# A two-layer hybrid trunk: block attention in pairs of heads with the values stationary, the r and k products first, the memory's keys of layer 0 projected inside the group norm

## What is computed

```python
# layer 0: RWKV-7 time mixing
dx = shift(h) - h
xr, xw, xk, xv, xa, xg = [h + dx * mu[s] for s in range(6)]
r = xr @ w_rkv[0]; k = xk @ w_rkv[1]; v = xv @ w_rkv[2]
w = -softplus(-(w0 + tanh(xw @ w1) @ w2)) - 0.5      # decay, low rank 64
a = sigmoid(a0 + (xa @ a1) @ a2)                      # rate, low rank 64
g = sigmoid(xg @ g1) @ g2                             # gate, low rank 128
o = scan over the tokens(r, decay, k, v, kk, a)       # 16 heads of 64
o = group_norm(o) * lnx_g + lnx_b                     # per head
x = x + ((o + bonus) * g) @ w_o
# both layers: cross-attention into 256 memory tokens, 4 heads of 256
kv = rms_norm(mem, ln_memkv[i]) @ w_kv                # keys and values
x = x + softmax(q k^T / 16) v @ w_o,  q = rms_norm(x, ln_mem[i]) @ w_q
# layer 1: block attention, 16 heads of 64, blocks of 256 tokens, rotary q and k
p = softmax(q k^T / 8, causal);  o = p v;  x = x + o @ w_o
```

## Time and profile before

| | us |
|---|---|
| median of 3 runs | 2491.16 (2490.17 to 2491.65) |
| the profiled execution's own time | 2486.15 |
| its span | 2484.3 |
| TensorE busy | 2130.0 (86%), mean granted clock 0.943 |
| VectorE busy | 621.0 (25%) |
| ScalarE busy | 413.8 (17%) |
| chain that ended last | PE 67%, DMA 21% (expert weights 19%), DVE 5%, issue of transfers 4%, ACT 1% |

### The profile page before, as it was taken

The page is one execution under the profiler, slowest core; times in us unless marked ns, Lnnn a source line. Parts: engine busy times, 40 slices in busy tenths (PEclk is TensorE's granted clock), DMA queues, the critical chain, the costliest instruction groups (busy, mean ns, idle before and its releaser), DMA issues.

```text
span 2484.3 us, 33316 instructions
## 1 busy us (share of the span) xinstructions
PE 2130.0 (86%) x14314; PEld 1120.0 (45%) x14314; DVE 621.0 (25%) x1388; ACT 413.8 (17%) x1003; POOL 198.4 (8%) x237
## 2 busy tenths in 40 slices
PE   6899999959999688778775999999999788877773
PEld 2345799935554422222222445766455322222221
DVE  5301655561022311000012420631022311000003
ACT  3202233320021011000001102621021010000001
POOL 1000121010000111111010000000000111111110
PEclk9999899979999799998898999999999899999997
DMA  4010000022324699999998122003324799999995
GB/s 137 34 68 34 11 4 4 4 85 71 132 71 169 240 401 404 406 402 409 409 403 341 35 97 73 1 26 110 119 71 167 310 402 405 408 406 408 396 410 212
DMA packets 113071, 515.08 MB, mean 207 GB/s; under 512 B 20736, under 2 KB 21896, under 8 KB 95536
## 3 DMA queue, kind: packets, MB, share of 16 engines
q1 hardware_dynamic: 101824, 496.34, 51.1%
q0 software_dynamic: 10880, 16.81, 2.1%
q10 hardware_dynamic: 240, 0.07, 0.0%
HBM read 503.73 MB, written 28.31 MB: 214 GB/s over the span
## 4 chain that ended last, share of the span: by engine, by line
PE 67%; DMA 21%; DVE 5%; SPq 4%; ACT 1%; issue 1%; POOLq 0%; DVEq 0%; POOL 0%; ACTq 0%
DMA big<-in_moe_w 19%; PE ps L1632 11%; PE ps L1645 11%; PE ps L2049 11%; PE ps L1740 9%; PE ps L1977 4%; SPq L471 4%; PE ps L2070 3%; PE ps L1691 2%; PE ps L1889 1%; PE ps L1881 1%; PE ps L1942 1%; PE ps L1854 1%; PE ps L1954 1%; PE ps L1860 1%
## 5 line engine op out<-in xcount | busy, mean ns | idle before, releaser
L2049 PE MATMUL ps<-big 128*64 128x512 f32 x2048 | 475.7, 618 | 73.7 <-DMA big<-in_moe_w 72.0
L2049 PEld LDWEIGHTS ps<-big 128*64 128x64 f32 x2048 | 163.0, 142 | 337.2 <-issue 326.2
L1632 PE MATMUL ps<-big 128*128 128x512 f32 (+1 forms) x768 | 279.4, 526 | 6.6 <-issue 6.6
L2070 PE MATMUL ps<-big 128*64 128x512 f32 x1024 | 255.9, 646 | 31.1 <-ACT big L1002 31.1
L1645 PE MATMUL ps<-big 128*128 128x512 f32 x640 | 275.5, 592 | 0.0
L1632 PEld LDWEIGHTS ps<-big 128*128 128x128 f32 x768 | 147.4, 193 | 136.8 <-issue 128.6
L1740 PE MATMUL ps<-big 64*64 64x64 f32 (+1 forms) x6144 | 203.1, 223 | 6.2 <-DVE big L1166 3.6
L1740 PEld LDWEIGHTS ps<-big 64*64 64x64 f32 x6144 | 198.1, 135 | 8.6 <-DVE big L1166 3.7
L1645 PEld LDWEIGHTS ps<-big 128*128 128x128 f32 x640 | 121.6, 190 | 151.3 <-issue 151.1
L1524 DVE SCALAR_TENSOR_TENSOR big<-big,ps 128x256 f32<-128x256 f32 x64 | 27.0, 422 | 530.2 <-ACT big L995 530.2
L2070 PEld LDWEIGHTS ps<-big 128*64 128x64 f32 x1024 | 73.4, 146 | 172.4 <-issue 134.1
(11 more groups left out here) (316 smaller groups left out, 1943.6 us busy)
## 6 DMA issues: line engine op xcount, KB each, us to landing
big<-in_moe_w SPq DMA_DIRECT2D x192, 2048.0 KB, 33.8
big<-in_mx_wkv SPq DMA_DIRECT2D x8, 2048.0 KB, 7.9
big<-in_rw_wrkv SPq DMA_DIRECT2D x6, 2048.0 KB, 8.0
big<-in_mb_wqkv SPq DMA_DIRECT2D x6, 2048.0 KB, 8.0
big<-in_mx_wq SPq DMA_DIRECT2D x4, 2048.0 KB, 7.9
big<-in_mx_wo SPq DMA_DIRECT2D x4, 2048.0 KB, 8.1
h_rows<-big SPq DMA_DIRECT2D x16, 512.0 KB, 12.5
big<-y_rows SPq DMA_DIRECT2D x8, 1024.0 KB, 8.2
```

The costliest lines, as they stand in the source:

```text
L1632: ins = mm(d[:, 0:n], lhsT=w[:, k, (j % 4) * P:(j % 4 + 1) * P], rhs=rhs[:, k, 0:n], start=k == 0, stop=k == KT - 1)
L2049: ins = mm(ps[2 + b][half * BR:(half + 1) * BR, :], lhsT=hgT[b][:, k], rhs=w13[set_][:, :, k, half * 256:(half + 1) * 256], start=k == 0, ...
L2070: ins = mm(ps[5 + b][half * BR:(half + 1) * BR, :], lhsT=hT[b][:, c0:c0 + BR], rhs=w2[set_][:, f, half * HB:(half + 1) * HB], start=f == 0 ...
```

## The change

1. **r and k first.** VectorE makes all five mixed inputs at once, in the order r, k, w, a, g, into R[0], R[2], R[3], R[4], R[5]. TensorE does the r and k products before the low-rank ones, and ScalarE's copies of them move to the front as well. SyncE issues loads 0 and 1 before the six low-rank loads. The `keep` mask of the scans moves from R[5] to R[2] and is written by VectorE before the first scan instead of by GpSimd at the start.
2. **The memory's keys of layer 0 in the group norm's gap.** The memory's tokens and the two halves of the key weights are loaded into R[0], R[3] and region 3 once VectorE has prepared chunk 7. Between chunks 6 and 7 ScalarE squares the memory and takes the root (`mem_std`), and VectorE scales it (`mem_scaled`). Behind the scan TensorE transposes it (now evacuated by ScalarE with the gain, before the squares of the group norm) and makes the keys (`xk`, evacuated by ScalarE behind the group norm's root), and only then the turns of the group norm. The keys lie in RE, so the router's four loads of layer 0 wait for the last memory scores.
3. **Block attention in pairs.** Score groups of both heads of a pair are issued side by side for each q, then both heads' turned weights for that q. The mask and the maximum become a minimum of keys scaled by -1/8, so the scaling instruction (L1286) is gone. VectorE copies the turned weights of q = 0 and 1, ScalarE those of q = 2 and 3. The values are made with v stationary (64 columns) and the turned weights moving (512 down to 128 columns), the two heads in the two halves of the output partitions of one bank, so the output is already turned; the reciprocal sums are spread over the partitions by eight more matmuls of 128 columns (`eb`), copied by ScalarE, and VectorE multiplies the two into HT. `moT` is gone.

```diff
-    o += norm(0) + [("hidden_wa",), ("hidden_g",)] + per("decay") + per("rate") + both("gate")
-    o += per("r") + per("k") + [("v", 0, t) for t in range(TT)] + [("knorm",)]
+    o += norm(0) + per("r") + per("k")
+    o += [("hidden_wa",), ("hidden_g",)] + per("decay") + per("rate") + both("gate")
+    o += [("v", 0, t) for t in range(TT)] + [("knorm",)]
     for t, scaled in enumerate(KSCALES):
         o += [("v", 1, t)] + ([("knorm_t",)] if t == 0 else []) + [("kscale", p) for p in scaled]
     o += [("bonus",)]
+    o += [("memT", 0, i) for i in range(KT // 2)] + per("xk", 0)
...
-            o += per("moT") + both("moba_out")
-        o += [("memT", l, i) for i in range(KT // 2)] + per("xk", l)
+            o += moba_order() + both("moba_out")
+        if l == 1:
+            o += [("memT", l, i) for i in range(KT // 2)] + per("xk", l)
...
+def moba_order():
+    scores = lambda p, q: [("ms", 2 * p + h, q) for h in range(2)] if p < PAIRS else []
+    turned = lambda p, q: [("mp", 2 * p + h, q) for h in range(2)]
+    values = lambda p: [("mo", p), ("eb", p)] if p >= 0 else []
+    o = [name for q in range(TT) for name in scores(0, q)]
+    for p in range(PAIRS):
+        for q in range(TT):
+            o += scores(p + 1, q) + turned(p, q) + (values(p - 1) if q == 1 else [])
+    return o + values(PAIRS - 1)
...
-        keep = tiles(R[5], KT)[:, KT - 1]
+        keep = region(8)[:, 0:T]
...
-        kxT = R[1][:, 0:2048].rearrange("p (k m) -> p k m", k=KT)
+        kxTs = [r[:, 0:2048].rearrange("p (k m) -> p k m", k=KT) for r in (RE, R[1])]
+        xk0_w = [tiles(r, KT) for r in (R[3], region(3))]
         vx = R[1][:, 2048:4096].rearrange("p (m n) -> p m n", m=MT)
-        memT = R[2][:, 0:2048].rearrange("p (k m) -> p k m", k=KT)
-        memn = R[2][:, 2048:4096].rearrange("p (m n) -> p m n", m=MT)
+        memTs = [r[:, 0:2048].rearrange("p (k m) -> p k m", k=KT) for r in (R[0], R[2])]
+        memns = [r[:, 2048:4096].rearrange("p (m n) -> p m n", m=MT) for r in (R[0], R[2])]
...
-        pm = R[5].rearrange("p (b q k) -> p b q k", b=2, q=TT)
-        pmT = RE.rearrange("p (b q k) -> p b q k", b=2, q=TT)
+        pm = [r.rearrange("p (h q k) -> p h q k", h=2, q=TT) for r in (R[5], region(1))]
+        pmT = [r.rearrange("p (h j q) -> p h j q", h=2, j=TT) for r in (RE, R[0])]
+        ebs = [R[1][:, i * T:(i + 1) * T] for i in range(2)]
...
-            for j in range(6):
+            load(0)
+            load(1)
+            sp.dma_start(lw1, rw_w1[0].rearrange("(k p) n -> p k n", p=P)).then_inc(lora_loaded, 16)
...
+            sp.dma_start(lg2, rw_g2[0]).then_inc(lora_loaded, 16)
+            for j in range(2, 6):
...
+            for g in range(2):
+                wait_dve(sp, g, CH - 1, "kappa")
+            load_mem(0)
+            for half in range(2):
+                sp.dma_start(xk0_w[half], mx_wkv[0, :, half * HB:(half + 1) * HB].rearrange("(k p) n -> p k n", p=P)
+                             ).then_inc(xk0_loaded[half], 16)
...
-                    sp.wait_ge(gn_done, GS)
+                    wait_filled(sp, ("xs", 0, XH - 1, 1))
...
+            def mem_std():
+                act.wait_ge(mem_loaded, 16)
+                for m in range(MT):
+                    A(memTs[0].rearrange("p k m -> p (k m)")[:, m * C:(m + 1) * C], memns[0][:, m], ACT.Square,
+                      accum_out=mss[:, m:m + 1]).then_inc(mem_sq, 1)
+                act.wait_ge(mvar_ready, 1)
+                A(mrstd[:], mss[:], ACT.Sqrt).then_inc(mstd_ready, 1)
+            def mem_keys_out(l):
+                for k in range(KT):
+                    wait_filled(act, ("xk", l, k))
+                    empties(A(kxTs[l][:, k], bank(("xk", l, k))[:, 0:M], ACT.Copy), ("xk", l, k))
...
+                if c == CH - 2:
+                    mem_std()
+            for i in range(KT // 2):
+                name = ("memT", 0, i)
+                wait_filled(act, name)
+                for h in range(2):
+                    k = 2 * i + h
+                    ins = A(memTs[0][:, k], bank(name)[:, h * M:(h + 1) * M], ACT.Copy, scale=col("ln_kv0", k))
+                empties(ins, name)
...
+            mem_keys_out(0)
...
+                    def exps(p, q):
+                        for hh in range(2):
+                            h, c0 = 2 * p + hh, hh * TT + q
+                            act.wait_ge(mmax_ready, 8 * p + 2 * q + hh + 1)
+                            if p >= 2 and q == 0:
+                                wait_filled(act, ("mp", 2 * (p - 2) + 1, TT - 1))
+                                act.wait_ge(msum_inv, p - 1)
+                            w = (q + 1) * P
+                            empties(A(pm[p % 2][:, hh, q, 0:w], bank(("ms", h, q))[:, 0:w], ACT.Exp, scale=-1.0,
+                                      bias=nmax[:, p % 2, c0:c0 + 1], accum_out=esum[:, p % 2, c0:c0 + 1]), ("ms", h, q))
+                    def spread(p):
+                        name = ("eb", p)
+                        if p >= 2:
+                            wait_emptied(act, ("mo", p - 2))
+                        empties(A(ebs[p % 2], bank(name)[:], ACT.Copy), name)
+                        exps(0, q)
+                    for p in range(PAIRS):
+                        for q in range(TT):
+                            if p + 1 < PAIRS:
+                                exps(p + 1, q)
+                            if q == 2 and p:
+                                spread(p - 1)
+                            if q >= 2:
+                                for hh in range(2):
+                                    name = ("mp", 2 * p + hh, q)
+                                    wait_filled(act, name)
+                                    empties(A(pmT[p % 2][:, hh, 0:q + 1, q * P:(q + 1) * P],
+                                              bank(name)[:, 0:(q + 1) * P].rearrange("p (j k) -> p j k", k=P), ACT.Copy), name)
+                    spread(PAIRS - 1)
...
-            mix(1, R[0])
-            mix(4, R[1])
-            mix(5, R[2])
+            mix(0, R[0])
+            mix(2, R[2])
+            mix(1, R[3])
+            mix(4, R[4])
+            mix(5, R[5])
             wait_emptied(dve, ("hidden_g",))
             V.tensor_scalar(hid_g, hid_g, 0.5, 0.5, ALU.mult, ALU.add).then_inc(hid_g_ready, 1)
-            mix(0, R[0])
-            mix(2, R[2])
...
+            def mem_scaled(l):
+                dve.wait_ge(mem_loaded, 16 * (l + 1))
+                if l == 0:
+                    dve.wait_ge(mem_sq, MT)
+                    V.tensor_scalar(mss[:], mss[:], 1.0 / C, RMS_EPS, ALU.mult, ALU.add).then_inc(mvar_ready, 1)
+                    dve.wait_ge(mstd_ready, 1)
+                    link(V.reciprocal(mrstd[:], mrstd[:]))
+                for m in range(MT):
+                    V.tensor_scalar(memns[l][:, m], memns[l][:, m], mrstd[:, m:m + 1], None, ALU.mult).then_inc(memn_ready, 1)
...
+                if c == CH - 2:
+                    mem_scaled(0)
...
+                    def mins(p, q):
+                        for hh in range(2):
+                            h, c0 = 2 * p + hh, hh * TT + q
+                            s = bank(("ms", h, q))
+                            wait_filled(dve, ("ms", h, q))
+                            if p >= 2 and q == 0:
+                                wait_emptied(dve, ("ms", 2 * (p - 2) + hh, TT - 1))
                             diag = s[:, q * P:(q + 1) * P]
                             link(V.tensor_tensor(diag, diag, m_causal[:], ALU.add))
+                            V.tensor_reduce(nmax[:, p % 2, c0:c0 + 1], s[:, 0:(q + 1) * P], AX, ALU.min
                                             ).then_inc(mmax_ready, 1)
 
+                    def weighted(p):
+                        name = ("mo", p)
                         wait_filled(dve, name)
+                        wait_emptied(dve, ("eb", p))
+                        empties(V.tensor_tensor(HT[:, p], bank(name)[:], ebs[p % 2], ALU.mult), name)
+                    for q in range(TT):
+                        mins(0, q)
+                    for p in range(PAIRS):
                         for q in range(TT):
+                            if p + 1 < PAIRS:
+                                mins(p + 1, q)
+                            if q < 2:
+                                for hh in range(2):
+                                    name = ("mp", 2 * p + hh, q)
+                                    wait_filled(dve, name)
+                                    empties(V.tensor_copy(pmT[p % 2][:, hh, 0:q + 1, q * P:(q + 1) * P],
+                                                          bank(name)[:, 0:(q + 1) * P].rearrange("p (j k) -> p j k", k=P)), name)
+                            if q == 1:
+                                for qq in range(TT):
+                                    for hh in range(2):
+                                        wait_emptied(dve, ("ms", 2 * p + hh, qq))
+                                if p >= 2:
```

(97 more changed lines are left out.)

186 lines of the change are left out of this document (38 added, 148 removed).

## The result

The changed kernel took 2461.85 us (median of 4 runs, 2460.39 to 2471.53) beside 2491.4 for the kernel before on the same chip: ratio 0.9893, 95% interval 0.9868 to 0.9919. The forecast was 2454, 2437 to 2466.

The account below looks back on a forecast made before the run. The prediction took a TensorE chain as the bound nearly throughout, with expert weight transfers late in both expert stages. Its terms, −8.4 − 31.8 + 3 = −37.2 us, took the median 2491.16 to 2454, range 2437 to 2466.

Parts of the forecast that it names:

- Part 1, -8.4: Start of the kernel: with r and k first, v starts at 181.8 instead of 190.2, 8.4 us won.
- Part 2, -31.8: Memory's keys in the group norm's gap: 33.9 us removed, 1.8 won before rwkv_out, 3.9 lost in the scan.
- The 5 MB of loads ... hide: Scan: loads of memory and key weights, issued a chunk before they are needed, cost no time.
- the norm between the chunks, 3.9: Scan, between chunks 6 and 7: the memory's squares, root and scaling hold TensorE up, 3.9 us lost.
- Part 3, +3: Block attention in pairs: 12.3 us per pair against 11.54, stage 103.5 against 100.2, so 3 us slower.
- I count one stretch at half clock: Block attention: gaps in the pair loop bring one half-clock stretch in the exposed values, 1.5 us lost.
- A: Rival, block attention: TensorE's array is the bound, 9.1 us per pair, stage 78, kernel 2429; chance 0.15.
- B: Rival, block attention: the two heads' scores do not overlap, +7 us, kernel 2461; chance 0.12.
- C: Rival, scan and gap: the memory's norm costs twice and the keys outlast the gap by 5 us, +9, 2463; chance 0.1.
- D: Rival: TensorE stays at half clock through block attention, 17.5 us per pair, +44, kernel 2495; chance 0.03.
- E: Rival, start: r and k first brings nothing, the gate copies' wait moving in front of v, 2462; chance 0.05.
- the 20 of the estimate: Block attention: by the skill's up to 2x alone, values and scores take half, the stage 20 us less.

Follow-up runs that it names:

- e4: The changed kernel with all three parts measured again, for a second profile: 2459.69 us, ratio 0.9866 to the kernel before.
- e1: The kernel before with only the r and k products moved first: 2482.3 us, ratio 0.9963 to the kernel before.
- e5: The changed kernel with ScalarE and VectorE emptying the banks of sums and values before the next pair's scores: 2448.4 us, ratio 0.9838 to the kernel before.
- e2: The kernel before with only the memory's keys of layer 0 moved into the group norm's gap: 2460.74 us, ratio 0.9876 to the kernel before.
- e3: The kernel before with only block attention in pairs: 2495.56 us, ratio 1.0026 to the kernel before.
- e8: The changed kernel without the pairs, block attention one head at a time as before: 2456.46 us, ratio 0.9875 to the kernel before.

## Why the prediction was right, and where it was not

- **The whole, -37.2.** By the ratios the change gave -26.7 (-32.9 to -20.2) at first and -33.4 (-38.1 to -28.6) in e4; the median of 2461.85 lies 8 us above the forecast 2454. The direction and most of the size come from terms that were right, as the next points show. Two steps were too cheap, by 5.7 us in part 2 and by 3.5 in part 3 (a stage of 107.0 us instead of 103.5). With both put in, the sum is -28.0.
- **Part 1, -8.4.** Measured -9.2. v's start, forecast 181.8, was between 181.1 and 182.4 in all nine profiles that have this part. It is the right mechanism in full: product lengths, the gate copies under the low-rank products, the sixth mixing as the last wait. In the changed kernel itself part of it was given back right behind v, in stretches at half clock: the scan's first level starts at 276.89 instead of 280.06 in the first profile, 3.2 us of 8.6. In e1 the scan kept its lead (first long stretch 281.17 instead of 290.03). Nothing in the code differs between them there, nor in e5, which kept its lead too (281.23), so it is chance of the clock.
- **Part 2, -31.8.** Measured -30.9 by e2's runs, but not by its own terms. The removal was exact: memory attention's output product starts 27.63 us earlier in the first profile (727.03 against 754.66) where rwkv_out started 6.26 later; 33.9, as forecast. The 1.8 won before rwkv_out came too: from the end of the scan to rwkv_out 37.8 us in both profiles, against 39.8. The router's loads cost nothing. Wrong was "**The 5 MB of loads ... hide**": for the queue they do, for TensorE they don't; +4.2 us in chunk 6 (31.6 against 27.4). Mis-sized was the norm between the chunks, 3.9: chunk 7 grew by 5.4 (32.1 against 26.7). The list of the work was right (squares 2.07, table 1.28, scaling 1.42 in the timeline): in the first profile VectorE's first copy comes at 489.06, which is 487.3 counted from the same start of the chunk, against 487.5 forecast. What the list lacked is what comes behind it: VectorE copies both groups' levels one after the other (0.75 us), and TensorE takes up its work at half clock. No rival named the loads. The loads' 4.2 and the norm's 5.4 are together 9.6 in place of 3.9.
- These 5.7 us do not appear in e2's ratio, and that it comes so near to -31.8 is luck: its interval reaches to -26.4. e2's profile does show them. Its first expert product starts at 825.24 instead of 854.12, 28.9 us earlier; 1.8 of these were there when chunk 6 began (448.08 against 449.85), for which part 2 does nothing, and 27.1 are part 2's. For the rest the reason may be the base, which is argued and not tested. The profiled execution of before was 5.0 under its median, and part of that is in the expert stages: from the first expert product to layer 1's query product it took 547.8 us, in the eleven others 549.2 to 551.8. A forecast by differences of one profile takes over such luck; I had moved it to the median whole, as if it scaled evenly.
- **Part 3, +3.** Measured +6.5 by e3 (+3.5 to +9.7). The loop was right to a tenth: 12.41 per pair at full clock against 12.3 forecast, with the very two stands that it named (1.9 and 0.7 to 1.1 us where it had 2.2 and 1.5), and values and sums at 2.30 and 0.87 against 2.2 and 0.9. Filling took 19.8 instead of 22, the last two pairs 19.2 instead of 18.5. The step that failed is "**I count one stretch at half clock**": three pairs of five had one, in sum 67.9 us instead of 61.5. The direction was in the earlier trace rows; I priced it by one stretch, though the loop's stands come back in every pair.
- **Rivals.** A (the array as the bound, 9.1 per pair) is refuted for this order, and nearly reached by another: in e5's stretch TensorE is busy 8.76 us of 10, which is 9.2 per pair of 10.53. B is refuted: scores of both heads overlap (four instructions of 384 columns in 0.92 us in TensorE's timeline, where end to end at 0.429 us per 512, they would take 1.29). C came true in part: the norm cost 5.4 instead of 3.9, but the keys did not outlast the gap, and the loads' 4.2 were not in it. D did not come: the clock came back in each pair or two. E is refuted by e1.
- **The Trainium skill.** Its page "TensorEngine Tiling (Array Packing)" has up to 2x under Theoretical Speedup and, under PSUM Bottleneck, that the emptying of banks is not sped up. The runs side with the second: with the same matmuls, only the order in which the banks are emptied changed, and the stage went from 107 to 91 us. Even then it is some 10 us under the one-head form, not the 20 of the estimate. Nor does the estimate follow from the factor alone, as it was said to: half of 2.35 and 2.18 us for each of 16 heads is 36 us. The 20 are what the eight pairs give at 9.1 instead of 11.5, with the sums' matmuls and the changes of shape counted in.

## What to carry to other kernels

When two readers empty banks that a faster TensorE fills, write their order by which bank is needed next, not by which result came first; follow one round of the loop with a clock in hand, and price its repeated stands a second time for the half clock that they bring. A small computation tucked between two steps of a serial loop stands on the path whole; split over the loop's own idle slots it was free here. Before you subtract from one profiled execution, look how it stands to its median, stage by stage if there is more than one profile.

## What was unexpected of the hardware

- A large load slows a stage of many small matmuls even when nobody waits for its data: 5 MB beside the scan cost about 4 us in a chunk of 27.4. Some 2.1 to 2.9 of them, where both stands come, are stands of TensorE of 1.0 to 1.5 us for which the profile names no releaser; in e8 half clock stood in the place of the second. What comes late is not shown. Eight pieces instead of two gave 65.7 us for both chunks, no less than the 63.7.
- Where the half clock falls differs between executions of the same code. The 64 small matmuls behind v took 10.70 us in one profile and 8.57 in the other.
- With the loop's stands cut from 1.9 and 0.7 to 1.1 us down to one of 1.1 in each pair, the clock stayed at 1.00 where it had fallen to 0.66. The change of two orders brought 16 us in the stage's profiles: about 1.9 in each of five pairs for the shorter loop, and about as much again in the three that had half clock. The runs' ratios say 7 to 14 (0.9838 against 0.9866 and 0.9893), the intervals being 4 to 6 us wide either way.
